# Normed tiles turned by transposing transfers, and attention queries regrouped by dilation on GpSimd, in a hybrid decoder layer on eight cores

## The chip, the cores and the metric

The kernel runs on 8 cores of one Trainium2 chip. Each core computes two of the 16 batch entries (b = 0, 1) from beginning to end with its own copy of the weights; the cores exchange nothing. The metric is the device time of the slowest core in microseconds. The engines of a core are called PE (TensorE: matmuls; PEld is its weight load), DVE (VectorE), ACT (ScalarE), POOL (GpSimd) and SP (SyncE, which here only issues DMAs). Each runs its own list of instructions in order and waits on semaphores for the others.

## The reference

For one layer, D = 1024, 2048 tokens a batch entry, feed-forward width 2816:

```
u = rms_norm(h) * (1 + scale1) + shift1        # per-batch scale and shift
h = h + 0.5 (1 + gate1) * (silu(u w1) * (u w3)) w2            # FFN 1
u = rms_norm(h) * (1 + scale2) + shift2
h = h + (1 + gate2) * token_mixing(u)                         # mixing
u = rms_norm(h) * (1 + scale3) + shift3
h = h + 0.5 (1 + gate3) * (silu(u w1') * (u w3')) w2'         # FFN 2
```

token_mixing projects u with w_in, then runs two branches. The attention branch has 12 heads of 64 in three groups; q and k are normed per head, and a query at t looks at t, t-d, t-2d, ... t-128d with d = 1, 4, 16 by group, with a bias linear in the distance. The other branch is chunked gated linear attention (GLA). Both are gated by sigmoids of projections of u, added, and projected with w_out.

## The kernel before

**Layout.** h (the residual) is [128, 16, 1024] f32 in SBUF, tokens on partitions, 16 tiles of 128 tokens. Every projection wants u with its 1024 features on partitions: u is [128, 8, 2048] bf16, feature chunk dc, then token. Four groups g of 512 tokens (four tiles each) are the unit in which u becomes ready, with keys ("u", g, dc).

**From h to u.** norm_tile (line 843) calls prep (line 802) for a tile: ACT squares and sums h, takes the reciprocal root, DVE writes the normed tile xn (128x1024 bf16) into one of four buffers given by xbuf (line 795), by tile number modulo 4. Two ticks later turn (line 816) runs: eight PE transposes (matmuls with ident_bf) of 128x128 into PSUM. A group holds four PSUM banks (of eight) from its first tile to its last; at its fourth tile, four operations of 128x512 on ACT and four on DVE read PSUM, apply the per-feature scale Amod and shift modT, and write u. ensure_u (line 631) makes the transposes due before the first use of a group. The layers are l = 0 (before FFN 1), 1 (mixing) and 2 (FFN 2), for both b.

- l = 1 is normed in the tail of FFN 1: its last part (lines 931 to 952) computes, for each of 16 tiles, two times six matmuls of 512 columns, adds to h on DVE, and calls norm_tile(1, ...) on the tile.
- l = 2 is normed in merge_out (line 1405), which runs two halves of 8 tiles: gates and branch projections, then w_out by two halves of columns; during the second half of columns each tile takes eight matmuls and is then normed.
- l = 0 of b = 1 is normed in the tail of FFN 2 of b = 0 (tail, line 1518): tiles 0 to 7 from a staged x, tiles 8 to 15 later, while FFN 1 of b = 1 has begun.

**Mixing.** mixing (line 1363) runs attention in six stages, STAGES = two head pairs ch by the groups with dilation 16, 4, 1. att_dense (line 984) makes a stage's q and k (projection of a group of 512 tokens, 8 matmuls; ACT squares, a matmul with the block-diagonal bd_bf sums per head, ACT makes the reciprocal root, DVE multiplies) and its v (16 units of 8 matmuls of 128 columns, whose stationary side is u at stride dil). att_core (line 1058) runs scores and the product with v. weave interleaves the core of a stage with att_dense of the next; the first att_dense of a batch runs alone. Buffers are doubled by p = stage modulo 2.

Two heads share the 128 partitions. To use 128 rows in every score matmul, q2[p] holds two copies of the queries, [128, 2, 2048]: in copy 0 the partitions 64 to 127 are zero, in copy 1 the partitions 0 to 63 are. In s2 (line 1007) DVE writes both heads to copy 0, copies partitions 64 to 127 to copy 1 and then zeroes them in copy 0; the zeros of copy 1 are written once per batch (line 1369). Queries stand in the order of tokens, so scores (line 1076) reads keys and queries with toks(dil, r, n), a slice of step dil: 128 tokens of step 16, 4 or 1 as the weights (keys), 128 or 256 queries as the moving side.

**Weights** come in f32 over SP's queue into two staging buffers stg, and are cast (most by POOL, some by DVE or ACT; the w2 and w_out ones are multiplied by the gate row in gsh) into slots wb. All DMAs but a few constants are issued by SP in one order. h tiles are loaded and y stored on the same queue.

**Order.** The order of the instructions on each engine is fixed when the program is built: Prog._order (line 139) walks the operations with estimated costs (_cost, line 100), looking ahead 48 units on PE, 24 on ACT and DVE, 6 on POOL, 8 on SP, and it also assigns PSUM banks. For a DMA on SP it takes 0.35 us plus 2.8 ns for each element of the source's leading dimensions as issue, its bytes over 300 GB/s one after another, and 2 us to land:

```
        if it["dma"] is not None:
            n = 1
            for s in kw["in_"].shape[:-1]:
                n *= s
            return 0.35 + n * 2.8e-3
...
                else:
                    bw = max(bw, st) + n / 300e3
                    done[k] = max(bw, free[e]) + 2.0
```

(in the second piece n is four bytes for each element of the destination). All instructions are emitted from one place, so the profile gives line L322 for nearly all of them; they are told apart by the names of their tiles. "arena" holds, by turns, the FFN's intermediate, its w2, q2, keys, values, the normed tiles of l = 1 and 2, and the GLA buffers; "t" is the t32 and t16 scratch (and the normed tiles of l = 0).

Of the kernel before, what the change touches and what calls it, by code (L numbers as in the profile page):

```python
# [8 lines left out]
BF16 = mybir.dt.bfloat16  # L9
# [3 lines left out]
P = 128  # L13
# [339 lines left out]
def build_nc(upto=99, dbg=False, nbr=NB):  # L353
# [29 lines left out]
    with es:  # L383
# [35 lines left out]
        sems = {e: es.enter_context(nc.semaphore(f"s_{e}")) for e in ("pe", "act", "dve", "pool")}  # L419
        dslots = ["pro", "stg0", "stg1"] + [f"h{i}" for i in range(16)] + [f"a{i}" for i in range(7)] + ["xt0", "xt1"]  # L420
        dsems = {s_: es.enter_context(nc.semaphore(f"d_{s_}")) for s_ in dslots}
# [9 lines left out]
        ident = t32[2][:, 0:P]  # L431
        stepsM = cst[:, 0:384]

        KB = 512
# [31 lines left out]
        Q_KEYS = [[("q", p, t) for t in range(NTS)] for p in range(2)]  # L466
        QZ_KEYS = [[("qz", p, t) for t in range(NTS)] for p in range(2)]
        K_KEYS = [[("k", p, t) for t in range(NTS)] for p in range(2)]
# [6 lines left out]
        MG_KEYS = [("mg", dc, t) for dc in range(DC) for t in range(2)]  # L475
        GD_KEYS = [("gd", t) for t in range(NTS)]

        def kc_view(w, c0, ncol):
            return w.rearrange("(kc p) f -> p kc f", p=P)[:, :, c0:c0 + ncol]

        def generate(pg, order):
# [320 lines left out]
            def prep(l, tt, src=None, sk=None):  # L802
# [11 lines left out]
                                                    op0=ALU.mult)), hk + [("rr", k)], [xk])  # L814

            def turn(l, b, tt):
                g, k = tt // 4, tt % 4
                if k == 0:
                    ubank[g] = [bank() for _ in range(4)]
# [164 lines left out]
            def att_dense(si_):  # L984
# [22 lines left out]
                def s2(nm, ts):  # L1007
                    pq, pqk, bi, i = pq_[(nm, ts)]
                    sl = slice(ts * TS, (ts + 1) * TS)
                    dst, gain = (q2[p][:, 0, sl], qg) if nm == "q" else (kb[p][:, sl], kg)  # L1010
                    pss, pssk, _ = bank()
                    mm(pss, bd_bf[:], sc[:, i, :], True, True, [("sc", i), "bdbf"], [pssk])
                    r32, rk = rstd_from(pss, pssk, 1.0 / 64)
                    pg.op("dve", ("scalar_tensor_tensor", dict(
                        out=dst, in0=pq, scalar=gain[:, 0:1], in1=r32[:],
                        op0=ALU.mult, op1=ALU.mult)), [pqk, rk, "smallT"], [(nm, p, ts)])
                    if nm == "q":
                        pg.op("dve", ("tensor_copy", dict(out=q2[p][64:128, 1, sl], in_=q2[p][64:128, 0, sl])),
                              [("q", p, ts)], [("qz", p, ts)])
                        pg.op("dve", ("memset", dict(ap=q2[p][64:128, 0, sl], constant=0.0)),  # L1020
                              [("qz", p, ts)], [("q", p, ts)])

# [35 lines left out]
            def att_core(si_):  # L1058
# [304 lines left out]
            def mixing(b):  # L1363
                GW.clear()
                pg.transfer(GLO_KEYS, ACC_KEYS)
                pg.transfer(GHI_KEYS, Q_KEYS[1] + QZ_KEYS[1] + K_KEYS[1])
                pg.transfer(GHI_KEYS + W2_KEYS, V_KEYS[1])
                pg.transfer(W2_KEYS, Q_KEYS[0] + QZ_KEYS[0] + K_KEYS[0])
# [12 lines left out]
                for i in range(6):  # L1381
                    core = att_core(i)
                    if i < 5:
                        weave(core, att_dense(i + 1))
                    else:
                        pg.transfer(Q_KEYS[0] + QZ_KEYS[0], GST_KEYS)
# [4 lines left out]
                pg.transfer(ACC_KEYS + Q_KEYS[1] + QZ_KEYS[1] + K_KEYS[1] + V_KEYS[1], OGLA_KEYS)  # L1391
                carry = []
# [102 lines left out]
            for b in range(nbr):  # L1495
# [4 lines left out]
                mixing(b)  # L1500
                pg.transfer(GD_KEYS, ["Gb"])
                make_Gb(1, b)
# [89 lines left out]
```

How the kernel before makes its waits and increments, by code:

```python
        def run(e, eng):  # L314
            for i in order[e]:
                it = ops[i]
                for s, v in waits[i]:
                    if s[0] == "e":
                        eng.wait_ge(sems[s[1]], count[(s[1], v)])
                    else:
                        eng.wait_ge(dsems[s[1]], 16 * (self.dcount[s[1]] if s[1] in self.group_slots else v))
                r = getattr(eng, it["fn"][0])(**it["fn"][1])
                if it["dma"] is not None:
                    r.then_inc(dsems[it["dma"][0]], 16)
                elif sig[i]:
                    r.then_inc(sems[e], 1)
            if e == "sp":
                for slot in final_waits:
                    if self.dcount.get(slot, 0):
                        eng.wait_ge(dsems[slot], 16 * self.dcount[slot])
```

## Time and profile before

| | us |
|---|---|
| runs, median (lowest to highest) of 3 | 3276.32 (3275.18 to 3480.48) |
| the profiled execution, device time | 3275.94 |
| its span on the slowest core (core 7) | 3274.3 |
| spans of the eight cores | 3268.7 to 3274.3 |
| mean granted TensorE clock, by core | 0.997 to 0.999 |

The profile is of one execution, and the rows further down are of its slowest core, core 7, with times in us from the start of its span. Durations of groups are ns of one instruction. A matmul's recorded duration overlaps with the next one, so the pace of a burst is read from start to start. FFN 1 of b = 0 ends near 538 us, its attention near 760, its GLA near 920, its merge near 1210, FFN 2 near 1680; b = 1 follows with FFN 1 to 2145, attention to 2360, and so on.

### The profile page before, as it was taken

How to read it: one execution, taken by the hardware profiler on the slowest of the kernel's cores; microseconds unless marked ns; L12 is line 12 of the kernel's file. 1: busy time of each engine (PE TensorE's matmuls, PEld its weight loads, DVE VectorE, ACT ScalarE, POOL GpSimd, SP SyncE). 2: the span in 40 equal slices, each digit the busy share in tenths (PEclk: the TensorE clock that was granted, in tenths of full speed). 3: DMA queues.
4: the chain of work that ended last, by engine and by line, in shares of the span. 5: the costliest groups of instructions: out<-in, count | busy, mean ns of one | idle time of the engine just before them, and what ended most of it. 6: DMA issues, size and time to landing. Idle time of an engine off the chain costs nothing.

```text
span 3274.3 us, 53515 instructions; the slowest of 8 cores (3268.7 to 3274.3 us)
## 1 busy us (share of the span) xinstructions
PE 3197.4 (98%) x18473; PEld 1636.2 (50%) x18473; DVE 1479.8 (45%) x2300; ACT 1132.4 (35%) x2194; POOL 781.5 (24%) x418
## 2 busy tenths in 40 slices
PE   4999999999999999999999999999999999999999
PEld 2444445666654444444454444456666444444444
DVE  3272327678754452323252323457776445422223
ACT  5201016777641431011351010377766223311100
POOL 1233222013424242121203120100143243231210
PEclk9999999999999999999999999999999999999999
DMA  9444334111125453232374131111211344341302
GB/s 297 147 155 134 111 106 121 46 54 53 53 66 166 130 179 103 65 103 65 132 229 142 39 116 33 39 40 35 66 53 56 113 141 156 116 142 52 103 14 103
DMA packets 280623, 333.33 MB, mean 102 GB/s; under 512 B 8450, under 2 KB 250616, under 8 KB 279336
## 3 DMA queue, kind: packets, MB, share of 16 engines
q1 hardware_dynamic: 279648, 329.41, 31.9%
q8 instruction: 156, 2.56, 0.3%
q14 instruction: 107, 0.88, 0.1%
q10 hardware_dynamic: 712, 0.49, 0.1%
HBM read 313.09 MB, written 16.78 MB: 101 GB/s over the span
## 4 chain that ended last, share of the span: by engine, by line
PE 92%; DVE 3%; DMA 2%; issue 1%; ACT 1%; SPq 0%; POOL 0%; DVEq 0%; ACTq 0%; POOLq 0%
PE ps L322 92%; DVE arena L322 2%; DMA arena<-w_mod 1%; DMA h<-x 1%; DVE t L322 1%; ACT u L322 0%; ACT t L322 0%; DVE sc L322 0%; ACT arena L322 0%; SPq L322 0%; ACT tiny L322 0%; POOL arena L322 0%; DMA y<-h 0%; DVE h L322 0%; POOL wb L322 0%
## 5 line engine op out<-in xcount | busy, mean ns | idle before, releaser
L322 PE MATMUL ps<-u,wb 128*128 128x512 bf16 x6912 | 1558.0, 380 | 17.4 <-POOL wb L322 5.9
L322 PEld LDWEIGHTS ps<-u,wb 128*128 128x128 bf16 x6912 | 670.4, 98 | 811.0 <-issue 36.0
L322 ACT ACTIVATE t<-ps 128x512 bf16<-128x512 f32 (+1 forms) x544 | 324.3, 598 | 1664.3 <-PE ps L322 1643.1
L322 PE MATMUL ps<-arena 128*128 128x512 bf16 (+2 forms) x3568 | 765.9, 363 | 5.6 <-DVE arena L322 2.0
L322 DVE TENSOR_TENSOR arena<-ps,t 128x512 bf16<-128x512 f32 x416 | 287.3, 691 | 954.5 <-PE ps L322 924.1
L322 POOL CAST wb<-stg 128x2048 bf16<-128x2048 f32 (+2 forms) x198 | 341.2, 1739 | 1319.4 <-PE ps L322 1204.9
L322 PEld LDWEIGHTS ps<-arena 128*128 128x128 bf16 x3568 | 345.8, 100 | 354.6 <-issue 8.7
L322 DVE TENSOR_TENSOR h<-ps,h 128x512 f32<-128x512 f32 x416 | 285.0, 690 | 330.1 <-PE ps L322 329.9
L322 PE MATMUL ps<-u,arena 128*128 128x512 bf16 x1600 | 352.0, 379 | 0.0
L322 POOL TENSOR_TENSOR arena<-stg,gsh 128x2048 bf16<-128x2048 f32 x40 | 180.7, 4519 | 576.7 <-PE ps L322 305.7
L322 PEld LDWEIGHTS ps<-u,arena 128*128 128x128 bf16 x1600 | 156.3, 98 | 187.1
L322 PE MATMUL ps<-wb,u 128*128 128x128 bf16 (+1 forms) x2560 | 230.8, 242 | 1.6 <-DVE t L322 0.6
L322 PEld LDWEIGHTS ps<-wb,u 128*128 128x128 bf16 x2560 | 195.2, 111 | 24.7 <-issue 7.2
L322 ACT ACTIVATE t<-t 128x512 f32<-128x512 f32 (+2 forms) x304 | 178.7, 615 | 35.6 <-DVE t L322 29.2
L322 PE MATMUL ps<-arena,wb 128*128 128x512 bf16 x640 | 159.0, 379 | 0.0
L322 POOL TENSOR_SCALAR arena<-arena,tiny 128x256 bf16<-128x256 f32 x120 | 113.3, 956 | 159.5 <-DVE arena L322 148.1
L322 DVE SCALAR_TENSOR_TENSOR t<-cst,ps 128x512 f32<-128x512 f32 (+1 forms) x160 | 101.2, 652 | 52.5 <-PE ps L322 35.2
L322 POOL CAST arena<-stg 128x2048 bf16<-128x2048 f32 x36 | 69.1, 1931 | 221.3 <-PE ps L322 149.2
L322 PE MATMUL ps<-wb,arena 128*128 128x512 bf16 x512 | 111.2, 379 | 0.0
L322 DVE TENSOR_TENSOR arena<-arena,t 128x512 bf16<-128x512 bf16 (+1 forms) x96 | 104.8, 1093 | 8.4 <-ACT t L322 1.5
L322 ACT ACTIVATE arena<-h 128x1024 bf16<-128x1024 f32 x64 | 67.5, 1056 | 117.3 <-DVE h L322 108.3
L322 PEld LDWEIGHTS ps<-arena,wb 128*128 128x128 bf16 x640 | 62.5, 98 | 74.1
(82 smaller groups left out, 1962.4 us busy)
## 6 DMA issues: line engine op xcount, KB each, us to landing
stg<-ffn_w SPq DMA_DIRECT2D x132, 1024.0 KB, 6.5
stg<-w_in SPq DMA_DIRECT2D x48, 1024.0 KB, 5.9
stg<-w_mod SPq DMA_DIRECT2D x29, 1024.0 KB, 6.8
stg<-w_in SPq DMA_DIRECT2D x52, 512.0 KB, 5.0
h<-x SPq DMA_DIRECT2D x32, 512.0 KB, 12.4
stg<-w_branch_gla SPq DMA_DIRECT2D x16, 1024.0 KB, 9.3
stg<-w_out SPq DMA_DIRECT2D x16, 1024.0 KB, 6.0
y<-h SPq DMA_DIRECT2D x32, 512.0 KB, 3.1
```

Of the source, the lines that this page charges most:

```text
L322: r = getattr(eng, it["fn"][0])(**it["fn"][1])
```

## The change

Both parts act on what stands before PE's matmuls.

**turn.** For every layer but l = 0 of b = 0, turn calls the new turn_dma. In place of eight PE transposes, SP issues one DMA with transpose=True from the normed tile (128x1024 bf16, 256 KB) straight into u[:, :, the tile's 128 tokens], with one of four new semaphores tr0 to tr3. The four transfers of a group write under keys ("ur", k), which take over from the group's readers. At the fourth tile the same eight operations (dc 0, 1, 4, 5 on ACT, the others on DVE) apply scale and shift, now in place in u. No PSUM bank is used. There are 5 x 16 = 80 such transfers.

**Queries.** s2 writes the normed queries of both heads to one of two small buffers qs (128x512 bf16, in the second half of gsh). Two POOL operations then write the two copies in q2[p]: each multiplies by a column of bd_bf (one on one head's 64 partitions, zero on the other's) and orders the queries by residue r, then by i (token = i*dil + r). DVE's copy, its memset and the memsets once per batch go, and so do the keys "qz". scores reads the queries as one contiguous slice; keys are still read with step dil.

```diff
+        qs = [gsh[:, 512 + 256 * i:768 + 256 * i].bitcast(BF16) for i in range(2)]
...
+            def turn_dma(l, b, tt):
+                g, k = tt // 4, tt % 4
+                xn, xk = xbuf(l, k)
+                if k == 0:
+                    pg.transfer([("u", g, dc) for dc in range(DC)], [("ur", i) for i in range(4)])
+                pg.dma(("dma_start", dict(out=u[:, :, tt * P:(tt + 1) * P], in_=xn, transpose=True)), f"tr{k}",
+                       reads=[xk], writes=[("ur", k)])
+                if k < 3:
+                    return
+                sl = slice(g * TS, (g + 1) * TS)
+                for dc in range(DC):
+                    rd = [("ur", i) for i in range(4)] + [("modT", l, 0, b), ("Amod", l, b)]
+                    A_, B_ = Amod[:, l, dc, b:b + 1], modT[:, l * 24 + dc, b:b + 1]
+                    if (dc // 2) % 2 == 0:
+                        pg.op("act", ("activation", dict(out=u[:, dc, sl], in_=u[:, dc, sl], func=AF.Identity,
+                                                         bias=B_, scale=A_)), rd, [("u", g, dc)])
+                    else:
+                        pg.op("dve", ("tensor_scalar", dict(out=u[:, dc, sl], in0=u[:, dc, sl], scalar1=A_, scalar2=B_,
+                                                            op0=ALU.mult, op1=ALU.add)), rd, [("u", g, dc)])
+
             def turn(l, b, tt):
                 g, k = tt // 4, tt % 4
+                if not (l == 0 and b == 0):
+                    turn_dma(l, b, tt)
+                    return
...
-                    dst, gain = (q2[p][:, 0, sl], qg) if nm == "q" else (kb[p][:, sl], kg)
+                    dst, gain = (qs[ts % 2], qg) if nm == "q" else (kb[p][:, sl], kg)
...
                     if nm == "q":
-                        pg.op("dve", ("tensor_copy", dict(out=q2[p][64:128, 1, sl], in_=q2[p][64:128, 0, sl])),
-                              [("q", p, ts)], [("qz", p, ts)])
-                        pg.op("dve", ("memset", dict(ap=q2[p][64:128, 0, sl], constant=0.0)),
-                              [("qz", p, ts)], [("q", p, ts)])
+                        w_ = TS // dil
+                        src = qs[ts % 2].rearrange("p (i r) -> p r i", r=dil)
+                        for hh in range(2):
+                            dv = q2[p][:, hh, :].rearrange("p (r i) -> p r i", r=dil)[:, :, ts * w_:(ts + 1) * w_]
+                            mk = bd_bf[:, hh * 64:hh * 64 + 1].unsqueeze(2).to_broadcast([P, dil, w_])
+                            pg.op("pool", ("tensor_tensor", dict(out=dv, in0=src, in1=mk, op=ALU.mult)),
+                                  [("qs", ts % 2), "bdbf"], [("q", p, ts)])
...
-                            mm(ps_[:, o:o + nq * P], kb[p][:, toks(dil, r, n)], q2[p][:, hh, toks(dil, r, n, nq * P)],
-                               True, True, [(nm, p, t) for nm in ("q", "qz") for t in tsof(dil, n, nq)] +
+                            mm(ps_[:, o:o + nq * P], kb[p][:, toks(dil, r, n)], q2[p][:, hh, (r * nb + n) * P:(r * nb + n + nq) * P],
+                               True, True, [("q", p, t) for t in tsof(dil, n, nq)] +
                                [("k", p, t) for t in tsof(dil, n)], [psk])
...
-                pg.transfer(["Gb"], GD_KEYS)
-                for p in (1, 0):
-                    pg.op("dve", ("memset", dict(ap=q2[p][0:64, 1, :], constant=0.0)), [],
-                          [("qz", p, t) for t in range(NTS)])
+                pg.transfer(["Gb"], GD_KEYS + QS_KEYS)
```

## Rows read from the trace of the kernel before

**Rows 1.** Page, part 1: busy us, share of the span, instructions.

```profile
PE 3197.4 (98%) x18473; PEld 1636.2 (50%) x18473; DVE 1479.8 (45%) x2300; ACT 1132.4 (35%) x2194; POOL 781.5 (24%) x418
```

**Rows 2.** Groups by form, whole span: busy us, mean ns, idle before, releasers.

```profile
L322 PE MATMUL ps<-u,wb 128*128 128x512 bf16 x6848 | 1542.9, 380 | 17.4 <-POOL wb L322 5.9 <-DVE u L322 2.9 <-DVE arena L322 2.6
...
L322 PE MATMUL ps<-arena 128*128 128x256 bf16 x456 | 101.0, 299 | 3.5 <-DVE arena L322 2.0 <-DVE t L322 1.5
...
L322 PE MATMUL ps<-ident_bf,arena 128*128 128x128 bf16 x896 | 68.5, 219 | 6.9 <-ACT u L322 3.9 <-DVE arena L322 2.8
...
L322 PE MATMUL ps<-arena 128*128 128x128 bf16 x296 | 57.5, 313 | 0.1
...
L322 PE MATMUL ps<-ident_bf,t 128*128 128x128 bf16 x256 | 19.6, 228 | 7.6 <-DVE t L322 7.4
```

**Rows 3.** Timeline, PE, end of the second FFN 1: start us, us, instruction.

```profile
2137.57 0.61 PE L322 MATMUL ps<-ident_bf,arena 128*128 128x128 bf16 x8
2138.02 2.75 PE L322 MATMUL ps<-arena 128*128 128x512 bf16 x12
2140.61 0.61 PE L322 MATMUL ps<-ident_bf,arena 128*128 128x128 bf16 x8
```

**Rows 4.** Timeline, PE: v projections, then scores at dilation 16, 4, 1.

```profile
594.80 1.50 PE L322 MATMUL ps<-wb,u 128*128 128x128 bf16 x24
...
596.25 2.08 PE L322 MATMUL ps<-arena 128*128 128x128 bf16 x8
598.15 0.52 PE L322 MATMUL ps<-t,arena 128*128 128x128 bf16 x6
...
614.19 1.08 PE L322 MATMUL ps<-arena 128*128 128x256 bf16 x4
615.09 0.52 PE L322 MATMUL ps<-t,arena 128*128 128x128 bf16 x6
...
639.26 0.60 PE L322 MATMUL ps<-arena 128*128 128x256 bf16 x4
639.70 1.89 PE L322 MATMUL ps<-u,wb 128*128 128x512 bf16 x8
```

**Rows 5.** Groups by form, PE, 615 to 640 us.

```profile
L322 PE MATMUL ps<-arena 128*128 128x128 bf16 x6 | 1.8, 297 | 0.0
```

**Rows 6.** Stretches: busy PE, PEld, DVE, ACT, POOL; PEclk, DMA share, GB/s.

```profile
540.00:560.00 20.00, 16.28 (x85) 7.67 (x84) 13.70 (x28) 12.72 (x24) 4.46 (x4) 0.91 0.60 145
585.00:597.00 12.00, 12.00 (x116) 8.34 (x115) 7.28 (x12) 10.72 (x18) 1.89 (x1) 1.00 0.33 87
622.00:640.00 18.00, 18.00 (x216) 14.19 (x214) 14.52 (x23) 11.18 (x21) 2.41 (x2) 1.00 0.32 89
1680.00:1690.00 10.00, 10.00 (x54) 4.81 (x53) 3.94 (x8) 4.59 (x8) 4.52 (x1) 1.00 1.00 332
```

**Rows 7.** Timeline, PE, first FFN 1 into mixing; [idle before].

```profile
541.33 0.61 PE L322 MATMUL ps<-ident_bf,arena 128*128 128x128 bf16 x8 [0.83 <-DVE arena L322]
541.77 1.89 PE L322 MATMUL ps<-u,wb 128*128 128x512 bf16 x8
...
547.00 3.36 PE L322 MATMUL ps<-u,wb 128*128 128x512 bf16 x8 [2.89 <-DVE u L322]
```

**Rows 8.** Groups by form, whole span: POOL and ACT.

```profile
L322 POOL TENSOR_TENSOR arena<-stg,gsh 128x2048 bf16<-128x2048 f32 x40 | 180.7, 4519 | 576.7 <-PE ps L322 305.7 <-DMA stg<-ffn_w 271.0
...
L322 ACT ACTIVATE u<-ps,modT,Amod 128x512 bf16<-128x512 bf16 x96 | 67.8, 778 | 36.9 <-PE ps L322 34.3 <-DVE Amod L322 2.5
```

**Rows 9.** DMA issues: KB each, median us to landing.

```profile
stg<-w_branch_att SPq DMA_DIRECT2D x16, 256.0 KB, 3.9
...
stg<-w_in SPq DMA_DIRECT2D x2, 64.0 KB, 2.4
```

**Rows 10.** Timeline, DVE, output projection of the first merge.

```profile
1194.80 0.69 DVE L322 TENSOR_TENSOR h<-ps,h 128x512 f32<-128x512 f32 x1 [1.04 <-PE ps L322]
1196.53 0.69 DVE L322 TENSOR_TENSOR h<-ps,h 128x512 f32<-128x512 f32 x1 [1.03 <-PE ps L322]
```

More of the change, by code:

```diff
@@ L419, in build_nc @@
         sems = {e: es.enter_context(nc.semaphore(f"s_{e}")) for e in ("pe", "act", "dve", "pool")}
-        dslots = ["pro", "stg0", "stg1"] + [f"h{i}" for i in range(16)] + [f"a{i}" for i in range(7)] + ["xt0", "xt1"]
+        dslots = ["pro", "stg0", "stg1"] + [f"h{i}" for i in range(16)] + [f"a{i}" for i in range(7)] + ["xt0", "xt1"] + [f"tr{i}" for i in range(4)]
         dsems = {s_: es.enter_context(nc.semaphore(f"d_{s_}")) for s_ in dslots}
@@ L466, in build_nc @@
         Q_KEYS = [[("q", p, t) for t in range(NTS)] for p in range(2)]
-        QZ_KEYS = [[("qz", p, t) for t in range(NTS)] for p in range(2)]
         K_KEYS = [[("k", p, t) for t in range(NTS)] for p in range(2)]
@@ L476, in build_nc @@
         GD_KEYS = [("gd", t) for t in range(NTS)]
+        QS_KEYS = [("qs", i) for i in range(2)]
         def kc_view(w, c0, ncol):
@@ L1015, in s2 @@
                         out=dst, in0=pq, scalar=gain[:, 0:1], in1=r32[:],
-                        op0=ALU.mult, op1=ALU.mult)), [pqk, rk, "smallT"], [(nm, p, ts)])
+                        op0=ALU.mult, op1=ALU.mult)), [pqk, rk, "smallT"], [("qs", ts % 2) if nm == "q" else (nm, p, ts)])
                     if nm == "q":
-                        pg.op("dve", ("tensor_copy", dict(out=q2[p][64:128, 1, sl], in_=q2[p][64:128, 0, sl])),
-                              [("q", p, ts)], [("qz", p, ts)])
-                        pg.op("dve", ("memset", dict(ap=q2[p][64:128, 0, sl], constant=0.0)),
-                              [("qz", p, ts)], [("q", p, ts)])
+                        w_ = TS // dil
[5 more added lines that the diff above has]
+                                  [("qs", ts % 2), "bdbf"], [("q", p, ts)])
                 items = [(nm, ts) for nm in "qk" for ts in range(NTS)]
@@ L1365, in mixing @@
                 pg.transfer(GLO_KEYS, ACC_KEYS)
-                pg.transfer(GHI_KEYS, Q_KEYS[1] + QZ_KEYS[1] + K_KEYS[1])
+                pg.transfer(GHI_KEYS, Q_KEYS[1] + K_KEYS[1])
                 pg.transfer(GHI_KEYS + W2_KEYS, V_KEYS[1])
-                pg.transfer(W2_KEYS, Q_KEYS[0] + QZ_KEYS[0] + K_KEYS[0])
-                pg.transfer(["Gb"], GD_KEYS)
-                for p in (1, 0):
-                    pg.op("dve", ("memset", dict(ap=q2[p][0:64, 1, :], constant=0.0)), [],
-                          [("qz", p, t) for t in range(NTS)])
+                pg.transfer(W2_KEYS, Q_KEYS[0] + K_KEYS[0])
+                pg.transfer(["Gb"], GD_KEYS + QS_KEYS)
                 pg.op("pool", ("memset", dict(ap=va[1][:, :, 64:128], constant=1.0)), [], V_KEYS[1])
@@ L1385, in mixing @@
                     else:
-                        pg.transfer(Q_KEYS[0] + QZ_KEYS[0], GST_KEYS)
+                        pg.transfer(Q_KEYS[0], GST_KEYS)
                         pg.transfer(K_KEYS[0] + V_KEYS[0], GSC_KEYS)
@@ L1390, in mixing @@
                 pg.transfer(V_KEYS[1], ON_KEYS)
-                pg.transfer(ACC_KEYS + Q_KEYS[1] + QZ_KEYS[1] + K_KEYS[1] + V_KEYS[1], OGLA_KEYS)
+                pg.transfer(ACC_KEYS + Q_KEYS[1] + K_KEYS[1] + V_KEYS[1], OGLA_KEYS)
                 carry = []
@@ L1500, in generate @@
                 mixing(b)
-                pg.transfer(GD_KEYS, ["Gb"])
+                pg.transfer(GD_KEYS + QS_KEYS, ["Gb"])
                 make_Gb(1, b)
```

## The prediction

> **What bounds the kernel now.** I read the page's busy times first: TensorE (PE) is busy for 3197.4 of 3274.3 us, DVE, ACT and POOL each for less than half [rows 1]. So the time is that of the matmul stream, and a change pays by what it takes out of that stream or out of its few holes. The groups by form then name the two kinds of matmul that the change touches, and what ended PE's idle time before them [rows 2]; the timelines give the pace of each, start to start, which the busy time of a burst blurs by the overlapped tail of its last matmul [rows 3 to 5]. Stretches show whether another engine is close behind PE there [rows 6].
>
> **Transposes off PE.** Five of the six norm layers (all but the first of batch 0) leave PE: 5 x 16 tiles x 8 = 640 of the 1152 identity matmuls [rows 2]. Eight of them take 0.45 us, start to start, in the middle of full work [rows 3]: 56 ns each, 640 x 0.056 = **35.8 us** out of the stream. Nothing hides them now, so the whole sum counts.
>
> They also bring waits. PE stood idle 6.9 us before transposes (for ACT and DVE writing u, and for normed tiles) and 2.9 us before projections for DVE's u [rows 2]. At the first passage from FFN 1 to mixing it waited 0.83 and 2.89 us and then ran eight matmuls in 3.36 us, against 1.89 us for the same eight before [rows 7]; the granted clock of that stretch is 0.91 [rows 6], so the wait cost a spell at 1.2 in place of 2.4 GHz, 1.5 us more. In all 6.9 + 2.9 + 1.5 = 11.3 us can come back: four PSUM banks are no longer held from a group's first tile to its last, and the two DVE memsets ahead of the evictions are gone.
>
> **What the transfers put in their place.** Tile k of a group goes out on SP when its normed tile is written; the eight u operations (four ACT, four DVE) need all four tiles. ACT's took 778 ns each out of PSUM [rows 8]; from bf16 in SBUF I count them the same, DVE's at nothing more, since no unit of PE starts earlier for it. The new price is the transfer itself, which no row shows. Bounds: at the rate of the busiest stretch, 332 GB/s [rows 6], 256 KB take 0.8 us. A 64 KB load cut into 1024 pieces of 64 B landed in 2.4 us [rows 9]; four times that, had the transfer to go in pieces as small, is 9.6 us. The nearest row is the 256 KB load of w_branch_att, 3.9 us to landing [rows 9], most of it latency that successive transfers share. I take 4 to 5 us to landing and 1.5 to 2.5 us of throughput per tile. The kernel's own planner orders the work as if SP needed 0.71 us, the data 1.75 us and the landing 2 us more (its cost formulas, not a measurement): 4.5 us, so the written order fits what I take.
>
> Where is it late? In the tail of FFN 1 a tile comes every 2.59 us (the twelve matmuls between two bursts [rows 3]) once the transposes are gone, in the output projection of a merge every 1.73 us for eight tiles [rows 10]. Four normed-tile buffers lie between, and PSUM's eight banks behind DVE. After FFN 1, PE still has six q and k projections over the first three groups before it needs the last group (6 x (1.73 + 0.22) = 12 us); the last tile needs about 3 us of ACT and DVE, 4 to 5 us of transfer and 1 to 3 us of u operations. That fits, with little to spare, and PE's order is fixed: every microsecond by which a transfer lands behind plan is a wait. After a merge and after FFN 2, eight tiles are done half a phase early. SP's queue is in order: behind a transfer that waits for its normed tile stand weight loads (those that POOL casts for the next projections), x loads and y stores; in the stretch at 1680 us the DMAs are busy all the time [rows 6], and a transfer there lands behind megabytes. I charge 2 x 3 us at the two FFN 1 to mixing passages, 3 x 1 us at the others: 9 us new waits less the 11.3 us that go, net **-2 us**, with bounds from -11 (none new) to +30.
>
> The Trainium skill (VectorE: DVE Perf Modes, "The three transpose paths") gives a 128x128 bf16 transpose 1309 ns through the DMA crossbar and advises TensorE where PSUM will do; eight of those would be 10.5 us a tile as an estimate, and that is the skill's case against this change. The same skill (DMA: Bandwidth & Descriptors, "Latency and other measured facts") gives transposing transfers 261 GB/s, which by an estimate is 1.0 us a tile. No row here decides between them; the time by the first stands with the third rival.
>
> **Queries regrouped.** Score matmuls read queries at stride dil. Start to start, 8 with dilation 16 took 1.90 us (238 ns each, 128 columns), 4 with dilation 4 took 0.90 us (225 ns, 256 columns), 4 with dilation 1 took 0.44 us (110 ns) [rows 4]; 128 plain columns take 56 ns [rows 3]. The weights (keys) stay strided, but v projections with strided weights run 24 in 1.50 us, 63 ns each or less [rows 4], so the price is the moving side's. The loops give 128 matmuls of 128 columns at dilation 16, 96 of 256 and 32 of 128 at dilation 4: 128 x 0.182 = 23.3 us, 96 x 0.115 = 11.0 us, and 32 x (297 - 219 ns) = 2.5 us [rows 2, 5]: **36.8 us** out of the stream.
>
> Not all of it ends the kernel sooner. Where dilation 16 runs, ACT is busy 10.72 of 12 us [rows 6]; without 16 x 0.182 = 2.9 of its 12 us of PE, it would need 9.1 us of PE against 10.7 of ACT. The planner can move work across, but I count half of the 23.3 there. At dilation 4 ACT has 11.18 of 18 us [rows 6] and the 13.5 us count in full. That makes 11.7 + 13.5 = **25 us**; bounds 10 and 37.
>
> Side costs. DVE loses a copy and a memset per query tile, POOL gets two products of 512 elements, 96 in all. POOL's product of 2048 f32 took 4519 ns [rows 8], 2.2 ns an element, so 1.1 us each at least; 2.2 us if the strided read halves its pace as it halves PE's. That is 106 to 211 us more of POOL in about 400 us of attention, in which it is busy a seventh of the time (1.89 of 12, 2.41 of 18 us [rows 6]): hidden, since the next stage's queries are made a stage ahead. Its cover is gone only at a batch's first stage, where eight products (9 to 18 us) follow the projections unwoven; behind them PE has k projections and 16 v units, about 15 us, and behind the products stand POOL's casts of the next weights. I charge 2 us for both batches.
>
> Sum against the profiled execution: -35.8 - 2 - 25 + 2 = -61 us on the stream; and DVE, which loses two operations per query tile, can close some of the holes before attention's matmuls (2.0 + 1.5 us before the scores [rows 2], as much elsewhere): -4. 3274.3 - 65 = 3209 us span. That execution was timed at 3275.9 us, the median of the runs is 3276.3: 2 us above the span, so **3211 us**, 2.0% faster. A measurement of this kernel can tell about 2% from no change: the line is at 3210.8 us.
>
> **Rivals.** (1) More comes back than I count: ACT's work spreads over the stages, all waits go. -35.8 - 36.8 - 11 + 2 = -82: 3194 us. For it: the mean ACT load of a stage is lower than in the stretch I quote (11.18 of 18 us); against: a fixed order planned on estimates. (2) Attention is bound by ACT, or waits for POOL, as soon as PE is shorter: the query part gives nothing, 3211 + 25 = 3236 us. (3) The other side: transfers go through at r us a tile. Loss beyond cover is 2 x (16 r - 54) us at the ends of FFN 1 (42 us of tail, 12 of cover) and 4 x (8 r - 20) at the merge halves (14 us of tiles, 6 of banks): 64 r - 188. It starts at r of 2.5 to 3.4 and makes the kernel over 2% slower than before from 64 r - 188 = 131, r = 5.0 us. At the upper bound of 9.6 us it costs 426 us: 3637 us. Small-piece loads speak against such an r (1024 pieces in 2.4 us [rows 9]), nothing shows the crossbar. At r = 3.5 it costs 36 us: 3247. By the skill's 10.5 us the same sum is 484 us, 3695 us. (4) The stride is not what slows the scores at dilation 4: then 13.5 us stay, 3224 us. The Trainium skill (Advanced Engine Details and Errata, "SBUF Cachelines") wants two hits on a 16-byte line for full pace, which a step of 8 B gives; the 225 against 110 ns [rows 4] disagree, so it gets little.
>
> **Chances.** The forecast and its neighbourhood (3200 to 3225) 0.42, half of it either side of the line; (1) 0.20; (2) 0.10; (4) 0.05; (3) with r from 2.7 to 5.0, same within 2%, 0.12; (3) above, slower, 0.11. So faster 0.41, within 2% 0.48, slower 0.11. The range takes (1) whole and (3) to r near 4: 3188 to 3290 us; the forecast's own is 3200 to 3225.
>
> **What would show it.** PE loses 640 identity matmuls and its dilation-16 scores fall from 419 to about 220 ns: else (4). SP shows the transposing transfers; their spacing at the end of FFN 1 says r, idle PE before u's projections released by ACT or DVE u says they are late. PE idle in attention released by ACT says (2), by POOL the products. I am wrong if PE's busy time falls by under 60 us, or if its idle time grows by over 15.

## The result, and the profile after

The changed kernel takes **3199.8 us** (median of four runs, 3197.9 to 3201.4), against 3276.3 us for the kernel before: a ratio of 0.977 with the interval 0.974 to 0.979, so 2.3% faster, by 76 us. The profiled execution took 3201.4 us with a span of 3198.8 us, 75.5 us below the span of before. The forecast was 3211 us, 2.0% faster, with more chance given to a difference within 2% (0.48) than to one above it (0.41). Where some executions of a kernel were disturbed, ratios and spans below are those of undisturbed ones.

The first lines of the page after (span; then busy us, share of the span, instructions):

```profile
span 3198.8 us, 52603 instructions; the slowest of 8 cores (3191.9 to 3198.8 us)
...
PE 3125.7 (98%) x17833; PEld 1587.3 (50%) x17833; DVE 1427.9 (45%) x2200; ACT 1130.0 (35%) x2198; POOL 897.7 (28%) x514
```

Against [rows 1], PE's busy time fell by 71.7 us and its idle time (span less busy) from 76.9 to 73.1 us, by 3.8. So the sum of the saving is nearly all busy time; how much of that is the order of the instructions rather than the edit is taken up further down. The groups by form of the whole span (busy us, mean ns, idle before and releasers) say which work:

```profile
L322 PE MATMUL ps<-u,wb 128*128 128x512 bf16 x6848 | 1541.7, 380 | 19.1 <-POOL wb L322 8.9 <-ACT u L322 1.9 <-ACT t L322 1.8
...
L322 POOL TENSOR_TENSOR arena<-gsh,bd_bf 128x512 bf16<-128x512 bf16 x96 | 110.0, 1159 | 87.6 <-DVE gsh L322 82.1 <-issue 0.2
...
L322 PE MATMUL ps<-arena 128*128 128x256 bf16 x456 | 86.7, 273 | 0.8 <-DVE t L322 0.5
...
L322 ACT ACTIVATE u<-u,modT,Amod 128x512 bf16<-128x512 bf16 x80 | 58.4, 802 | 14.4 <-DMA u<-t 7.3 <-DMA u<-arena 7.0
...
L322 DVE TENSOR_SCALAR u<-u,Amod,modT 128x512 bf16<-128x512 bf16 x80 | 41.0, 571 | 3.1 <-DMA u<-arena 3.1
...
L322 PE MATMUL ps<-arena 128*128 128x128 bf16 x296 | 32.0, 222 | 0.4 <-ACT t L322 0.3 <-DVE arena L322 0.2
L322 PE MATMUL ps<-ident_bf,arena 128*128 128x128 bf16 x384 | 30.4, 219 | 0.0
```

Beside [rows 2]: the two rows of transposes, 896 and 256 instructions, are down to 384 here, all GLA's, and 128 from t, the one layer that PE still turns. The 128-column row fell from 313 to 222 ns a piece, 26.9 us over its 296 (23.3 + 2.5 were counted), the 256-column one from 299 to 273, 11.9 us over its 456 (11.0 counted, for the 96 at dilation 4). The new POOL row, 96 products of 1.16 us, is the regrouping; ACT's operations on u take 802 ns from SBUF, where they took 778 from PSUM [rows 8]. PE's waits before projections did not go (19.1 us against 17.4). The timeline of PE at a dilation-16 stage (start us, us, instruction) shows the pace start to start:

```profile
570.82 1.15 PE L322 MATMUL ps<-arena 128*128 128x128 bf16 x16
571.81 0.38 PE L322 MATMUL ps<-sc,bd_bf 128*128 128x512 bf16 x1
```

Sixteen scores in 0.99 us, 62 ns each, where before they took 238 [rows 4]. The transfers, as the view of DMA issues has them (median us from issue to landing; 256 KB each):

```profile
u<-arena SPq DMA_TRANSPOSE x64, 3.9
u<-t SPq DMA_TRANSPOSE x16, 6.8
```

### The profile page after: what moved, and what is told of

Same layout as the page of the kernel before. It is cut to its first block, busy times and chain, and to the rows that moved or that the text cites. A ratio compares the mean times of both kernels' runs of the same rounds, so it can differ in the third digit from the quotient of the medians.

```text
span 3198.8 us, 52603 instructions; the slowest of 8 cores (3191.9 to 3198.8 us)
## 1 busy us (share of the span) xinstructions
PE 3125.7 (98%) x17833; PEld 1587.3 (50%) x17833; DVE 1427.9 (45%) x2200; ACT 1130.0 (35%) x2198; POOL 897.7 (28%) x514
## 4 chain that ended last, share of the span: by engine, by line
PE 89%; DMA 4%; ACT 2%; DVE 2%; issue 2%; POOL 1%; SPq 1%; DVEq 0%; ACTq 0%; POOLq 0%
PE ps L322 89%; DMA stg<-ffn_w 2%; DMA stg<-w_mod 2%; ACT t L322 1%; DVE arena L322 1%; SPq L322 1%; DMA u<-arena 1%; ACT arena L322 0%; ACT u L322 0%; POOL wb L322 0%; DVE t L322 0%; POOL arena L322 0%; DVE u L322 0%; DVE gsh L322 0%; ACT sc L322 0%
## 5 line engine op out<-in xcount | busy, mean ns | idle before, releaser
L322 PE MATMUL ps<-u,wb 128*128 128x512 bf16 x6912 | 1556.8, 380 | 19.1 <-POOL wb L322 8.9
L322 PE MATMUL ps<-arena 128*128 128x512 bf16 (+2 forms) x3568 | 723.3, 353 | 3.4 <-POOL arena L322 2.1
L322 PEld LDWEIGHTS ps<-arena 128*128 128x128 bf16 x3568 | 339.3, 100 | 352.9 <-issue 7.0
L322 ACT ACTIVATE t<-t 128x512 bf16<-128x512 f32 (+2 forms) x304 | 177.5, 613 | 26.6 <-DVE t L322 20.2
L322 POOL TENSOR_TENSOR arena<-gsh,bd_bf 128x512 bf16<-128x512 bf16 x96 | 110.0, 1159 | 87.6 <-DVE gsh L322 82.1
```

Source lines behind the costliest of these rows:

```text
L322: r = getattr(eng, it["fn"][0])(**it["fn"][1])
```

## The experiments

Each was timed in turns with the kernel before on its chip. "Planner's setting" is the pair (spare, tie) with which Prog._order writes the order: spare is how many PSUM banks must stay free if a unit that opens one is to be taken ahead of its turn, tie by how many us longer the chain behind a unit must be for it to go ahead of an equally early one. make_plan tries nine pairs and keeps the one with the lowest estimate.

### One part at a time

Transfers alone: queries as before.

```
+ turn_dma and its call in turn, semaphores tr0..tr3
  s2, scores, keys: as before
```

> The transposing transfers alone, queries as before. Theory A (both parts act on a stream that TensorE bounds, and add up): 35.8 us of transposes and about 2 us of waits go, 3276 - 38 = 3238 us, ratio 0.988. Rival P (the transfers' u operations on VectorE are slowed only where GpSimd's query products run beside them): without those products every u operation on VectorE takes the 0.34 us that four of them take when alone, against a mean of 571 ns in the changed kernel, and the passage from FFN 1 to mixing has less idle TensorE, so up to 5 us more is gained, 3233 us. If the u operations stay at 571 ns on average, rival P falls.

Ratio 0.984 (0.982 to 0.985), 3222.0 us: 54 us less, more than theory A (3238) or rival P (3233) gave. The stream alone gives 35.8, so PE's waits fell by far more than "net -2": its idle time is 64.3 us, 12.6 below before's 76.9. Rival P's other sign is not there either: DVE's operations on u still take 528 ns on average, up to 3.88 us, without any of POOL's query products.

Queries alone: transposes as before.

```
- if not (l == 0 and b == 0): turn_dma(l, b, tt); return
```

> The queries regrouped alone, transposes on TensorE as before. Theory A: the whole 36.8 us of the stream ends the kernel sooner, with up to 4 us of small holes: 3236 to 3240 us, ratio 0.988. Rival H (the step of the prediction: ScalarE becomes the bound where dilation 16 runs, so that half of its 23.3 us stays): 3276 - 25 - 4 + 2 = 3249 us, ratio 0.992.

Ratio 0.989 (0.988 to 0.991): 35 us less, the whole 36.8 us of stream within the interval. The halving of dilation 16's part (0.992) fell here: PE's busy time is 34.5 us lower and its idle time 77.4 us against 76.9, and in the attention of batch 0 PE waited 1.3 us for ACT in all (0.7 us before), so the saving did not turn into waits for ACT.

### Is it the stride?

Queries made by POOL as in the change, but stored and read in token order.

```
- dv = q2[p][:, hh, :].rearrange("p (r i) -> p r i", r=dil)[:, :, ts * w_:(ts + 1) * w_]
+ dv = q2[p][:, hh, sl].rearrange("p (i r) -> p r i", r=dil)
- q2[p][:, hh, (r * nb + n) * P:(r * nb + n + nq) * P]
+ q2[p][:, hh, toks(dil, r, n, nq * P)]
```

> As the run with the queries alone, but GpSimd writes the two copies in the order of tokens and the scores read them at stride dil as before: what is left is VectorE freed of a copy and a memset per query tile and GpSimd's 96 products. Theory A (the gain is the moving side's pace): ratio 0.999 to 1.001, scores at 419 ns for dilation 16. Rival D (much of the gain is VectorE's relief): 10 us or more are gained, ratio 0.997 or less.

Ratio 1.002 (1.001 to 1.004): a little slower than before, above theory A's range too, and rival D's 10 us are not there. make_plan writes this kernel with the same setting as the kernel before and the queries alone (the setting is explained under the planner below), so the order is not what differs. The groups by form, first of this kernel, then of the queries alone:

```profile
L322 POOL TENSOR_TENSOR arena<-gsh,bd_bf 128x512 bf16<-128x512 bf16 x96 | 151.2, 1659 | 100.7 <-DVE gsh L322 95.3
...
L322 PE MATMUL ps<-arena 128*128 128x256 bf16 x456 | 101.1, 299 | 1.8 <-DVE t L322 1.6
...
L322 PE MATMUL ps<-arena 128*128 128x128 bf16 x296 | 57.6, 313 | 1.2 <-POOL arena L322 1.1
```

```profile
L322 POOL TENSOR_TENSOR arena<-gsh,bd_bf 128x512 bf16<-128x512 bf16 x96 | 109.2, 1150 | 95.8 <-DVE gsh L322 90.1
...
L322 PE MATMUL ps<-arena 128*128 128x256 bf16 x456 | 88.7, 272 | 1.7 <-DVE t L322 1.6
...
L322 PE MATMUL ps<-arena 128*128 128x128 bf16 x296 | 31.9, 222 | 0.1
```

With the same engine making the same products, only the step between the queries differs, and the scores are as slow as before (299 and 313 ns). So the pace is the stride's, at dilation 4 too, which is the only one whose matmuls of 256 columns have a step: their common mean falls by 27 ns. The Trainium skill (Advanced Engine Details and Errata, "SBUF Cachelines") asks for two hits on a 16-byte line for full pace; at dilation 4 a step of 8 B gives that, and the row says half pace, so here the measurement decides against it. Writing with a step costs POOL too, 1659 against 1150 ns. Moving DVE's work to POOL without the regrouping gains nothing and costs some 8 us.

### Price and cover of the transfers

Each transposing transfer issued twice, the second once the first has landed.

```
+ for _ in range(2):
      pg.dma(("dma_start", dict(out=u[:, :, tt * P:(tt + 1) * P], in_=xn, transpose=True)), ...
```

> The changed kernel with every transposing transfer issued twice, the second after the first has landed, so that SP needs about 1.3 + 2.6 + 1.3 = 5.2 us for each tile and a tile lands about 5 us later. The rival of the prediction with slow transfers: 64 x 5.2 - 188 = 145 us of loss, 3345 us, ratio to the kernel before 1.02. Theory A with a better cover than that formula counts (the order is planned anew with the longer transfer, weight loads move out of the way): under 70 us of loss, ratio below 1.0.

3275.9 us, on a single execution: 76 us above the change, between the two forecasts (under 70, and the 145 of the third rival's sum), and equal to before. PE's timeline at the first FFN 1 to mixing passage, where the brackets give the idle time before:

```profile
540.61 5.35 PE L322 MATMUL ps<-u,wb 128*128 128x512 bf16 x16 [11.13 <-ACT arena L322]
...
557.42 3.00 PE L322 MATMUL ps<-u,wb 128*128 128x512 bf16 x6 [7.57 <-ACT u L322]
```

PE now waits 11.13 and 7.57 us there, 5.61 and 8.42 us between FFN 2 and FFN 1, 5.68 and 10.04 at the second passage to mixing; the mean granted clock of that core fell to 0.987. With one transfer the longest waits at these places are 2.09, 0.89 and 1.42 us. So a tile's transfer is covered once, not twice. The 76 us are not the transfers' alone, though. make_plan found no order for this kernel under any setting with spare 1, nor under (2, 40) and (2, 1e9), and took (3, 40), with an estimate of 3277.2 us; for the change it estimates 3193.1 us with its own setting and 3203.4 with (3, 40). By these estimates some 10 us belong to the setting, and on the chip each of the two GLA stretches, in which no transfer runs, is 4 us longer than in the change. At the first passage SP took 40.3 us for 18 transfers and the weight loads between them (501.53 to 541.83 us), 4.5 us a tile in place of the 5.2 expected.

What one costs shows in the change itself: SP issues them 1.22 us apiece at the least, back to back 1.3 us apart (below, three in 3.92 us), 2.5 to 4 us beside other traffic and once 8.65. Between 500 and 545 us the DMA engines are full in the change (share 1.05, 222 GB/s) where they had a share of 0.43 before. In the last group before mixing the first operation on u starts 3.4 us after the issue (2104.68, 2108.08). The timeline of SP in the changed kernel, where the second FFN 2 norms begin:

```profile
2617.89 3.92 SPq L322 DMA_TRANSPOSE u<-arena  x3
2621.97 0.45 SPq L322 DMA_DIRECT2D stg<-w_in  x1
2622.52 2.77 SPq L322 DMA_TRANSPOSE u<-arena  x1
```

The forecast took 1.5 to 2.5 us of throughput and 4 to 5 us to landing; both came out at or just below the lower end. The Trainium skill (VectorE: DVE Perf Modes, "The three transpose paths") has 1309 ns for one 128x128 block through the crossbar; here eight blocks in one transfer were issued every 1.3 us, so that figure is not to be multiplied by blocks.

### What the planner did with the change

The two parts alone give 54 and 35 us less, together 76, not 89, and the transfers alone give more than they take off PE. The programs differ in more than the parts: for the kernel before, and for the queries alone, make_plan takes (1, 40); for the change and the transfers alone (2, 1e9). So that pair was set by hand:

```
- ps = [self._order(spare, tie) for spare in (1, 2, 3) for tie in (3.0, 40.0, 1e9)]
+ ps = [self._order(2, 1e9)]        (before; queries alone)
+ ps = [self._order(1, 40.0)]       (change; transfers alone)
```

> The kernel before, not one operation changed; only its order is the planner's second setting (two spare banks, no priority), which it chooses by itself for the changed kernel and for the transfers alone, in place of the first (one spare bank, priority above 40 us), which it chooses for the kernel before and for the queries alone. Theory O (part of the measured gain is the order, because the stretches of gated linear attention, in which nothing was changed, are 5.7 us shorter per batch with the transfers and not with the queries alone): about 11 us are gained, ratio 0.9965. Rival (the shorter stretches come from what the transfers leave free, DMA or banks): ratio 1.000 or above. The planner's own estimate for this order is 8.7 us longer than for the other.

Ratio 0.9991 (0.998 to 1.0001): for the kernel before the new setting is worth about 3 us, and the interval reaches from nothing to 6.5. Theory O's 0.9965 lies outside it.

> The changed kernel in the planner's first setting, which the kernel before has. Theory O: 11 us of the gain are lost, 3211 us, ratio to the kernel before 0.980. Rival (the transfers do it): 0.977 as the changed kernel.

Ratio 0.9837 (0.9824 to 0.985), 3222.1 us: for the changed kernel it is worth 22 us, more than either theory gave it.

> The transfers alone, as in e1_turn_only, but with the planner held to the setting that it takes for the kernel before (spare 1, tie 40). Known with that setting: neither part 3276.8, queries alone 3240.3, both 3222.1 us. Theory O (within one setting the two parts simply add; what looked like overlap between them came from comparing kernels of different settings): 3276.8 less the 18 us by which the transfers lowered 3240.3 to 3222.1, so 3259 us, ratio 0.994 to 0.996. Rival N (the parts overlap under any setting: both give TensorE room at the same passages, so alone each saves more than on top of the other): the transfers alone then save their 35.8 us of stream less some waits, about 3241 to 3246 us, ratio 0.989 to 0.991.

> The queries alone, as in e2_query_only, with the planner held to the setting that it takes for the changed kernel (spare 2, tie 1e9). Known with that setting: neither part 3274.6, transfers alone 3222.0, both 3199.8 us. Theory O (the parts add within one setting): 3274.6 less 22.2, so 3252 us, ratio 0.992 to 0.993. Rival N (they overlap under any setting): the queries alone save their whole 36.8 us of stream, 3238 us, ratio 0.988.

All eight combinations of two settings and four sets of parts, as ratio to the kernel before, PE's busy and idle time from the page, and the time at the lower granted clock after the first 100 us of the span (added up from the trace's clock records):

```
setting     parts        ratio (95%)             us less  PE busy  PE idle  half clock
(1, 40)     none         1                          0     3197.4    76.9      3.4
(1, 40)     transfers    0.996  (0.9944-0.9975)    13     3170.8    88.4     34.1
(1, 40)     queries      0.9893 (0.9878-0.9907)    35     3162.9    77.4      7.9
(1, 40)     both         0.9837 (0.9824-0.985)     53     3132.1    88.1     20.5
(2, 1e9)    none         0.9991 (0.998-1.0001)      3     3198.4    74.5     17.1
(2, 1e9)    transfers    0.9835 (0.9821-0.985)     54     3156.8    64.3     10.2
(2, 1e9)    queries      0.9896 (0.9882-0.9909)    34     3164.6    75.4     22.2
(2, 1e9)    both         0.9768 (0.9744-0.9791)    76     3125.7    73.1     17.1
```

The queries are worth 35 us alone and 40 beside the transfers with the old setting, 31 and 22 with the new one. The transfers are worth 13 and 18 us with the old, 51 and 42 with the new: their value hangs on the order in which the rest is written. Theory O held with the old setting (3259 expected; the profiled execution took 3261.1) and missed with the new one (3252 expected, 3242.0 measured), where the parts overlap by some 9 us and the queries alone came nearer to rival N's 3238. That is near the width of the intervals, but the traces show the same 9 us and where they lie. With the new setting the queries shorten the way to the end of batch 0's attention by 13.6 us beside the transfers and by 16.7 without them, and the way from there past the FFNs to the end of batch 1's attention, leaving GLA and merge out, by 9.8 and 16.2 us. Most of the loss is thus at batch 1's passage into mixing, where PE's idle time in attention goes from 6.9 us (transfers alone) to 11.9 and the time at the lower clock from 3.4 to 6.8 us.

Like for like, with the setting (2, 1e9) and the same 17.1 us at the lower clock, PE's busy time falls from 3198.4 to 3125.7: 72.7 us, where 72.6 were counted.

Where the 38 us between the two kernels with transfers alone lie (spans 3259.2 and 3221.1) was read by cutting both spans at the same instructions of PE: the first bd_bf matmul of each mixing, its last product with v, the last matmul of the GLA branch (out of sc and t, with the merge begun), the last of the merge.

```
stretch                                    old setting   new setting   difference
FFNs and norms between the two mixings        965.7         949.9        -15.8
attention of batch 1                          226.9         215.5        -11.4
GLA and the start of the merge, b 0 and 1   2 x 204.2     2 x 200.3       -7.8
the rest                                                                  -3.1
```

The first is one place. PE's timeline there with the old setting, with idle time and releaser in brackets, and of ACT and DVE at the same place:

```profile
1698.41 2.53 PE L322 MATMUL ps<-u,arena 128*128 128x512 bf16 x8 [2.12 <-ACT t L322]
1701.95 3.57 PE L322 MATMUL ps<-u,arena 128*128 128x512 bf16 x8 [1.01 <-DVE arena L322]
1706.41 3.52 PE L322 MATMUL ps<-u,arena 128*128 128x512 bf16 x8 [0.89 <-ACT t L322]
1710.95 1.24 PE L322 MATMUL ps<-u,wb 128*128 128x512 bf16 x5 [1.01 <-DVE arena L322]
...
1696.37 1.28 ACT L322 ACT_TABLE_LOAD   x1 [6.95 <-PE ps L322]
...
1701.11 0.69 DVE L322 TENSOR_TENSOR arena<-ps,t 128x512 bf16<-128x512 f32 x1 [10.76 <-PE ps L322]
```

ACT had nothing for 6.95 us and DVE for 10.76, both waiting for PE; then PE waits for them, ten times about 1 us, and the granted clock drops to the lower level for 10.2 us of this stretch: 11.7 us idle in all against 1.3 with the new setting. The same passage with the new setting:

```profile
1685.52 3.62 PE L322 MATMUL ps<-u,arena 128*128 128x512 bf16 x16
1689.52 3.61 PE L322 MATMUL ps<-u,arena 128*128 128x512 bf16 x16 [0.39 <-ACT t L322]
1692.97 1.24 PE L322 MATMUL ps<-u,wb 128*128 128x512 bf16 x5
```

In the kernel before the old order runs without these waits (0.49 and 0.55 us at 1673 and 1678 us). So the old setting, good for the kernel before, writes a worse order once the transposes are out. The new one, with the transposes in, gives back at the merges what it gains elsewhere; PE's timeline at the first merge of the kernel before with the new setting:

```profile
1081.47 1.08 PE L322 MATMUL ps<-ident_bf,arena 128*128 128x128 bf16 x12 [0.40 <-ACT u L322]
1084.88 0.61 PE L322 MATMUL ps<-ident_bf,arena 128*128 128x128 bf16 x8 [2.33 <-DVE arena L322]
1085.32 0.59 PE L322 MATMUL ps<-arena,wb 128*128 128x512 bf16 x2
```

Transposes wait 2.33 us for normed tiles, likewise 1.37 and 1.69 us at 1209 to 1212 us and 2.20 us at 2686 us, and in each of the two merges the clock is at the lower level for 3.4 us. Counted from the last matmul out of arena and sc, each merge is 7 us longer (253.3 us against 246.3 in batch 0), and GLA up to there 5.6 us shorter (161.7 against 167.3). With the transfers the new order has none of these waits: those transposes are not on PE's queue any more. Why the old setting bunches PE's work at 1690 us was not traced further.

A third setting, (2, 40), in the changed kernel:

> The changed kernel with a third setting of the planner (spare 2, tie 40), whose own estimate is 3202.4 us, between 3206.9 for the setting of before (3222.1 us on the chip) and 3193.1 for the chosen one (3199.8 us). Theory E (the estimate orders the settings rightly, and the chip stretches its differences 22.3/13.8 times): 3193.1 to 3202.4 is 9.3, times 1.6, so 3215 us, ratio 0.981. Rival F (what costs on the chip is that only one bank is held spare, spare 1; with two the transposes' freed banks are used whatever the tie): 3200 to 3204 us, ratio 0.977.

Ratio 0.980 (0.9787 to 0.9814), 3211.8 us: between the two theories, nearer E. Its stretch between the mixings is the 949.9 us of spare 2, its GLA, counted to the last matmul out of arena and sc, the 168 us of tie 40 (161.6 with 1e9). So, by these two stretches, spare 2 takes the waits at 1690 us away and tie 1e9 shortens GLA.

### Two tries at the waits that are left

In the change PE still waits about 24 us beyond its first 200 us, and the largest piece, 6.6 us, is the second passage from FFN 1 to mixing. Timelines of POOL, DVE and PE at the second one:

```profile
2103.91 7.35 POOL L322 TENSOR_TENSOR arena<-gsh,bd_bf 128x512 bf16<-128x512 bf16 x5 [10.53 <-DVE gsh L322]
...
2108.08 5.52 DVE L322 TENSOR_SCALAR u<-u,Amod,modT 128x512 bf16<-128x512 bf16 x4
...
2109.79 0.38 PE L322 MATMUL ps<-u,wb 128*128 128x512 bf16 x1 [1.21 <-ACT u L322]
2110.49 1.08 PE L322 MATMUL ps<-u,wb 128*128 128x512 bf16 x4 [0.33 <-ACT u L322]
2111.90 0.38 PE L322 MATMUL ps<-u,wb 128*128 128x512 bf16 x1 [0.33 <-ACT u L322]
2112.45 0.38 PE L322 MATMUL ps<-u,wb 128*128 128x512 bf16 x1 [0.17 <-DVE u L322]
2113.75 0.38 PE L322 MATMUL ps<-u,wb 128*128 128x512 bf16 x1 [0.93 <-DVE u L322]
2114.96 0.58 PE L322 MATMUL ps<-sc,bd_bf 128*128 128x512 bf16 x1 [0.84 <-ACT sc L322]
2116.96 0.58 PE L322 MATMUL ps<-sc,bd_bf 128*128 128x512 bf16 x1 [1.42 <-ACT sc L322]
```

Four operations on u take DVE 5.52 us beside POOL's products, where four took 1.37 us at 2096.67 us, when POOL stood still. PE waits five times for u and twice for sc after it, and the granted clock is at the lower level for 6.8 us from 2114.8. Two edits aim at it: the products of a batch's first stage on DVE, and the last group of a normed layer turned by PE again.

```
- pg.op("pool", ("tensor_tensor", dict(out=dv, in0=src, in1=mk, op=ALU.mult)),
+ pg.op("dve" if si_ == 0 else "pool", ("tensor_tensor", ...
```

> The changed kernel, with the eight query products of each batch's first attention stage on VectorE in place of GpSimd, order setting as in the changed kernel. Theory P (VectorE's in-place u operations, SBUF to SBUF in bf16, stand still while GpSimd's products run: four took 5.5 us in place of 1.6 at the second passage from FFN 1 to mixing, which costs idle TensorE and a spell at half clock): 4 to 8 us gained on the changed kernel, ratio 0.9745 to 0.976, and no u operation of that passage over 0.6 us. Rival L (the late landing and ScalarE's queue set the passage): within 2 us of the changed kernel, 0.977.

```
- if not (l == 0 and b == 0):
+ if not (l == 0 and b == 0) and not (l == 1 and g == 3):
      turn_dma(l, b, tt)
```

> The changed kernel, with the last group of four tiles before mixing turned by TensorE as in the kernel before (2 x 32 transposes back, 3.6 us of stream), order setting as in the changed kernel. Rival L (the transfer's latency, about 4 us from issue to landing after the last tile, sets the passage): idle TensorE and half clock go, 9 us per pair of passages less 3.6 us: 5 us gained, ratio 0.975. Theory P: the u operations read PSUM and do not meet GpSimd either, so the same 5 us; against both, if the passages are set by ScalarE's queue of norms: 3 us lost, 0.978.

Ratios 0.9764 (0.9749 to 0.9779) and 0.9773 (0.976 to 0.9786): neither differs from the change. The first took the stretching away (DVE's four take 1.37 us) and left attention of batch 1 with 11.9 us of idle PE, as in the change: the wait moved to other releasers. In the second that stretch is 8.2 us shorter, but the one before it is 6.2 us longer; in batch 0 the same trade is 2.9 us shorter against 4.1 longer. Of the first edit's forecasts, theory P's gain of 4 to 8 us did not come (its span is 3198.8 us, as the change's, though the interval touches P's 0.976), and rival L's "no gain" stands. Of the second's, both theories' gain of 5 us (0.975) lies outside the interval, and the loss of 3 us (0.978) lies in it, which was to come if ACT's queue of norms sets the passage. The trace of the change agrees with that one: the last four transfers before mixing are issued at 2091.24, 2095.62, 2099.46 and 2104.68 us, each less than 0.15 us after its normed tile was written, and the last tile's squares start on ACT only at 2101.17 us, right behind four operations on u (2098.35 to 2101.27). The transfer itself is the last 3.1 us of that chain (landed at 2107.74). No run took work off ACT there, so this is read from the trace and not shown by an edit.

## Why the prediction was right or wrong

**What leaves the stream: right.** 35.8 + 36.8 = 72.6 us were counted. PE's busy time fell by 71.7, and by 72.7 between two kernels of the same setting; with the old setting on both sides it fell by 65.3, with 17.1 us more at the lower clock in it. Dilation-16 scores came down to 62 ns, where 56 was taken.

**"Not all of it ends the kernel sooner": wrong, and this is the step that failed.** Half of dilation 16's 23.3 us was withheld because ACT would bind. The windows after (busy PE, PEld, DVE, ACT, POOL; clock, DMA share, GB/s) do show ACT as full as that step feared:

```profile
585.00:600.00 15.00, 14.67 (x155) 10.12 (x153) 6.93 (x11) 14.60 (x25) 1.96 (x2) 1.00 0.34 93
680.00:700.00 20.00, 20.00 (x149) 11.64 (x147) 9.97 (x14) 19.09 (x34) 10.12 (x10) 1.00 0.20 53
```

But PE is full as well. That the planner, which looks ahead 48 units on PE, put other stages' work beside ACT's is the likely reason; it was not tested apart. [rows 6] gave 10.72 of 12 us for ACT in one stretch, and the step read it as that stage's limit, while over the whole attention of that batch ACT was busy 167 of 214 us, and 169 of 199 after the change. The queries alone gave 35 us: all of the 34.5 us of busy time ended the kernel sooner, and idle time grew by 0.5 where 11.7 were withheld. With 36.8 in place of 25, the forecast's own sum is 3199 us.

**The waits: right in the sum by luck.** -2, +2 and -4 us were expected, -3.8 came. But the working assumed the order as before and late transfers as the danger. With the order as before, waits and half clock grow (88.1 us idle, both parts, against 76.9), and the change would be worth 53 us, not 76. The freed banks were counted as a wait saved at their place (part of the 11.3 us); what was not thought of is that the planner, with them and the transposes gone, picks another setting, worth 22 us here. With the old one the result is 3222, 11 us above the forecast in place of 11 below. So that the corrected sum of 3199 meets the result is luck too: it leaves out 11 us of new waits under the old order, and the better order that takes them away again.

**The transfers: right.** 1.3 us apart and 3.9 us to landing, where 1.5 to 2.5 and 4 to 5 were taken: a little too dear, and near enough. The third rival, with r of 5 us and more, fell. Its formula is not well tested: the run with every transfer twice was expected at an r of 5.2 (145 us) and ran at some 4.5 us a tile at the first passage, for which the sum gives 100; it lost 76, part of it by another setting. Where the loss starts, at an r of 2.5 to 3.4 by the formula, no run shows.

**DVE's relief (-4): not there as a sum.** The 3.5 us before the scores of 256 columns [rows 2] are 0.8, but PE's idle time over the attention of both batches, 12.2 us before, is 18.3, most of the growth at the second passage; and POOL's products without the regrouping gained nothing. **POOL's products (+2):** 1.16 us each, as its lower bound of 1.1 said; eight of them at a batch's first stage stretch DVE's work, but moving that stage's products to DVE gains nothing.

**Rivals.** (1), all of both savings, at 3194 us, is nearest in mechanism, at 5.8 us from the result; (2) fell with the queries alone; (4) fell with the queries in token order. The time lies inside the wide range and 0.2 us below the forecast's own (3200 to 3225). The forecast stood on the line of 2%, and the 11.7 us that were withheld put it on the side of "within 2%", where the measured interval, 2.1 to 2.6% faster, is not.

## What to carry to other kernels

When a schedule is written by a program, a change moves the order of everything: plan both kernels under both settings before putting down a gain or a loss to the edit itself, since an edit can be worth 13 us in one order and 51 in another, as the transfers were here. If the planner is free to choose, look which setting each variant got before reading a difference. A stretch in which another engine is nearly full need not bound a stage if the schedule can bring work from its neighbours; look at the share over the whole phase as well (here ACT's 167 of 214 us). And a strided moving operand is paid on every read: here 110 us of regrouping on POOL, which had the room, took 35 us off the engine that sets the time.

## What the runs showed of the hardware

- 128 bf16 columns as the moving side with a step of 32 B between them went through in 238 ns a matmul, with none in 62; 256 with a step of 8 B in 225 against 110. The keys, which are the weights of the same matmuls, kept their step of 32 B, and 62 ns is the pace all the same.
- A DVE operation on u, SBUF to SBUF, 128x512 bf16, took 0.40 us at its median in the changed kernel and 0.57 on average. All 13 of the 80 that took over 0.45 us ran beside an operation of POOL (products, casts, a memset), and none of the others did. Each of the 13 ended 0.14 to 0.15 us after an operation of POOL had: the longest, 2764.02 to 2766.57 us, after a product that ended at 2766.43.
- POOL's product of two 128x512 bf16 operands took 1.16 us, 1.66 when its output had a step between elements too.
- A transposing transfer of a 128x1024 bf16 tile from SBUF to SBUF: 1.22 us of issue, 1.3 us apart, 3.9 us to landing at the median and 6.8 where x loads and stores ran beside it.
- Where PE had waited for 1 to 3 us in several pieces close together, its granted clock was at 1.2 GHz for 3.4 to 10.2 us at a time, 34 us in all in the worst of the eight combinations; where it waited 11.13 us in one piece and more behind it, in the run with doubled transfers, the mean granted clock between 500 and 560 us was 0.84.
